# Gate and up products of two feed-forward stages as seven half-size products each, with Pool making one weight sum and the gated product

## The reference, cut to what matters

```python
h = h + mix @ w_out[l]                    # 512x1024 @ 1024x1024
hn = rms_norm_2(h, ffn_norm[l])
gu = hn @ w_gate_up[l]                    # 512x1024 @ 1024x5632
h = h + (jax.nn.silu(gu[..., :D_FF]) * gu[..., D_FF:]) @ w_down[l]
```

## Time and profile before

| | |
|---|---|
| median of 3 runs | 3445.44 us (3439.52 to 3446.58) |
| the profiled execution: its own time | 3438.87 us |
| its span, first to last instruction | 3437.1 us (1.8 us lie around it) |
| TensorE busy, DVE busy, ACT busy, Pool busy in it | 89%, 40%, 32%, 7% |
| mean granted TensorE clock | 0.958 of full |
| the two feed-forward stages | about 2240 to 2700 us and 3020 to 3437 us of the span |

### The profile page before, as it was taken

One profiled execution on the slowest core, in us unless ns is written; L12 is line 12 of the kernel. 1 busy time (PEld: TensorE's weight loads), 2 busy tenths in 40 slices (PEclk: granted clock), 3 DMA queues, 4 the chain that ended last, 5 costly groups with the idle time before them and its releaser, 6 DMA issues. The chain is left out here.

```text
span 3437.1 us, 44411 instructions
## 1 busy us (share of the span) xinstructions
PE 3069.4 (89%) x17561; PEld 2178.1 (63%) x17561; DVE 1387.9 (40%) x2258; ACT 1115.5 (32%) x1938; POOL 250.7 (7%) x278
## 2 busy tenths in 40 slices
PE   7999999999698878887887698889999998889999
PEld 5777888878533333333333485868888775778887
DVE  6872566663430000000000467553332467553332
ACT  4672666762200000000000435432222336332222
POOL 0000332210000000000000000300000000300000
PEclk9999999999899999999999799999999998999999
DMA  5322222234699999999998520023333320023332
GB/s 135 89 76 80 74 68 68 74 91 136 251 379 429 429 429 429 430 429 429 429 429 357 157 74 13 6 93 98 96 95 104 94 57 1 20 92 96 98 98 92
DMA packets 361295, 612.37 MB, mean 178 GB/s; under 512 B 73952, under 2 KB 308224, under 8 KB 336384
## 3 DMA queue, kind: packets, MB, share of 16 engines
q1 hardware_dynamic: 351152, 598.72, 47.3%
q0 software_dynamic: 9216, 8.42, 0.7%
q10 hardware_dynamic: 720, 2.36, 0.2%
HBM read 605.23 MB, written 23.07 MB: 183 GB/s over the span
## 5 line engine op out<-in xcount | busy, mean ns | idle before, releaser
L268 ACT ACTIVATE f_hi<-f_raw 128x1024 fp32r<-128x1024 f32 x148 | 156.6, 1059 | 516.2 <-PE ff_bk L328 516.0
L1888 PE MATMUL ex_up<-ex_W,ex_XT 128*64 128x512 f32 x1024 | 249.9, 644 | 76.2 <-DMA ex_W<-in_w_expert_up_dram 76.2
L1888 PE MATMUL ex_gp<-ex_W,ex_XT 128*64 128x512 f32 x1024 | 241.3, 625 | 59.2 <-DMA ex_W<-in_w_expert_gate_dram 57.8
L326 PE MATMUL ff_bk<-h_b_hi,f_hi 128*128 128x512 f32 x704 | 276.1, 392 | 2.8 <-DVE h_b_lo L3860 2.8
L327 PE MATMUL ff_bk<-h_b_lo,f_hi 128*128 128x512 f32 x704 | 275.5, 391 | 0.0
L328 PE MATMUL ff_bk<-h_b_hi,f_lo 128*128 128x512 f32 x704 | 275.3, 391 | 0.0
L277 DVE TENSOR_TENSOR f_lo<-f_raw,f_hi 128x1024 fp32r<-128x1024 f32 x148 | 180.5, 1223 | 208.4 <-ACT f_hi L268 208.0
L1917 PE MATMUL ex_yp<-ex_W,ex_hT 128*64 128x512 f32 x1024 | 228.5, 598 | 34.3 <-DMA ex_W<-in_w_expert_down_dram 21.8
L1931 DVE TENSOR_TENSOR ex_hid<-ex_sg,ex_up 128x512 f32<-128x512 f32 x32 | 22.0, 688 | 580.7 <-PE ex_up L1888 580.7
L1888 PEld LDWEIGHTS ex_up<-ex_W,ex_XT 128*64 128x64 f32 x1024 | 89.6, 147 | 235.7 <-issue 235.7
L1888 PEld LDWEIGHTS ex_gp<-ex_W,ex_XT 128*64 128x64 f32 x1024 | 88.0, 144 | 211.3 <-issue 209.5
(11 more groups left out here) (612 smaller groups left out, 6305.8 us busy)
## 6 DMA issues: line engine op xcount, KB each, us to landing
ex_W<-in_w_expert_up_dram SPq DMA_DIRECT2D x64, 2048.0 KB, 37.6
ex_W<-in_w_expert_down_dram SPq DMA_DIRECT2D x64, 2048.0 KB, 38.4
ex_W<-in_w_expert_gate_dram SPq DMA_DIRECT2D x64, 2048.0 KB, 37.6
b_raw<-in_w_in_dram SPq DMA_DIRECT2D x88, 512.0 KB, 3.8
f_raw<-in_w_gate_up_dram SPq DMA_DIRECT2D x88, 512.0 KB, 3.7
f_raw<-in_w_down_dram SPq DMA_DIRECT2D x44, 512.0 KB, 3.5
m_raw<-in_w_in_dram SPq DMA_DIRECT2D x20, 512.0 KB, 4.1
m_early<-in_w_in_dram SPq DMA_DIRECT2D x20, 512.0 KB, 4.0
```

What stands on the lines that cost most here:

```text
L268: a.activation(self.hi[n % self.SLOTS][:, to], self.raw[n % self.RAW][:, at], ACT.Copy).then_inc(self.cast, 1)
L326: pe.matmul(out, a[0], b[0], start=first, stop=False)
L1888: ins = pe.matmul(ps[part[e], :], XT[b][:, q, part[e]], row_view(slots[e], KD)[:, q, :], start=(q == 0), stop=(q == KD - 1))
```

## The change

The product of the turned tokens and the weights of one block is seen as a 2x2 by 2x2 product: tokens in halves of 256 and features of the input in halves of 512 on one side; on the other side the upper and lower half of the gate tile and of the up tile. Winograd's form of Strassen's method makes it from seven products of half size (p1 to p7) in place of eight. The product of a half is 4 rows-of-128 times `mm3`, 12 matmuls with 256 tokens moving; a block takes 7 x 12 = 84 matmuls of 256 columns.

New work for it:

- On the token side, once a stage: 14 groups of four transposes (`turn_middle(g)`) and 14 pairs `turned_hi`, `turned_lo` in place of 8, and two calls of `make_sums` (on DVE; each one subtraction over 1024 columns and two `scalar_tensor_tensor` over 512, with drains).
- On the weight side, per block u (a gate tile and an up tile): four sums of 512 columns (s3, s2, s4 on DVE, s1 on Pool), all with both inputs in SBUF, and splits of three 1024-column pairs (the gate tile, Q1, Q3) and of one 512-column tile (s2): four ACT casts and four DVE subtractions.
- After the products of block u: `keep` (ACT copies the 256 columns of p1 out of PSUM) and `join` (DVE: four additions out of PSUM, of 512, 256, 512 and 512 columns, with three drains), then `Silu` on ACT and the gated product on Pool (`gate_f`), 512 columns, both inputs in SBUF, into `raw_f`.
- The split of f (`make_f_hi`, `make_f_lo`, 22 of each) moves from the gate phase into the down phase, four of them ahead of the first down tile; the down tiles for the first column half are taken in the order `FIRST_DOWN`, and the signs of the last adds change (`ALU.subtract`).
- Gate and up tiles no longer go through `Stream` but through `GateWeights`, with four raw buffers; its loads wait for the split that frees the buffer.
- Pool's instructions wait only for their operands.

The diff, cut to its core:

```diff
+class GateWeights:
+    RAW = 4
+        order = [("p1", 0), ("p2", 0), ("p7", 0), ("p6", 0), ("p3", 0), ("p4", 0), ("p1", 1), ("p5", 0)]
+        for u in range(1, units):
+            order += [(n, u + (n == "p1")) for n in ("p7", "p6", "p3", "p2", "p1", "p4", "p5") if u + (n == "p1") < units]
+    def operand(self, n, u):
+        pair, half = {"p1": (self.g_slots[u % 2], 0), "p2": (self.g_slots[u % 2], 1), "p7": (self.q1, 0), "p3": (self.q1, 1),
+                      "p5": (self.q3, 0), "p4": (self.q3, 1), "p6": (self.s2, 0)}[n]
+    def load(self, sp, g):
...
+            sp.wait_ge((self.q1_split, self.q3_split)[g % 2], u - 1)
+    def sum_s3(self, v, u):
...
+        v.tensor_tensor(g[:, 0:T], g[:, 0:T], up[:, 0:T], ALU.add).then_inc(self.s3_ready, 1)
+    def sum_s1(self, p, u):
+        p.wait_ge(self.s3_ready, u + 1)
+        p.tensor_tensor(up[:, 0:T], up[:, 0:T], up[:, T:], ALU.add).then_inc(self.s1_ready, 1)
+    def sum_s2(self, v, u):
+        if u > 0:
+            self.wait_used(v, "p6", u - 1)
+        v.drain()
+        v.tensor_tensor(self.s2_sum(u)[:], g[:, 0:T], up[:, T:], ALU.add).then_inc(self.s2_ready, 1)
+    def sum_s4(self, v, u):
+        v.tensor_tensor(g[:, T:], g[:, T:], self.s2_sum(u)[:], ALU.add).then_inc(self.s4_ready, 1)
+    def g_hi(self, a, u):
+        self.wait_loaded(a, 2 * u)
...
+            self.wait_used(a, "p2", u - 2)
...
+    def q1_hi(self, a, u):
+        a.wait_ge(self.s4_ready, u + 1)
...
+            self.wait_used(a, "p3", u - 1)
...
+    def q3_hi(self, a, u):
+        a.wait_ge(self.s1_ready, u + 1)
...
+            self.wait_used(a, "p5", u - 1)
...
+    def s2_hi(self, a, u):
+        a.wait_ge(self.s2_ready, u + 1)
...
 def stage_ffn(...)
   TensorE
-                for m in range(BLOCKS):
-                    for j in range(2):
...
-                        for q in range(KD):
-                            ins = mm3(pe, bk[4 + 2 * j + m % 2][:], W.tile(n, q), both(h, q), q == 0, q == KD - 1)
+                def gate_product(n, u):
...
+                    for q in range(4):
+                        at_q = slice(q * P, (q + 1) * P)
+                        ins = mm3(pe, out, (hi[:, at_q], lo[:, at_q]), both(hc[n], q), q == 0, q == 3)
+                    ins.then_inc(G.used, 1)
+                for n, u in G.order:
+                    if u == 0 and n == "p7":
+                        for g in range(4, 8):
+                            turn_middle(g)
+                    elif u == 0 and n in ("p6", "p3", "p4"):
+                        for g in {"p6": (8, 9), "p3": (10, 11), "p4": (12, 13)}[n]:
+                            turn_middle(g)
...
+                    gate_product(n, u)
   ACT
+                for u in range(BLOCKS - 1):
+                    if u > 0:
+                        G.q3_hi(a, u)
+                        gate_silu(u - 1)
+                    G.s2_hi(a, u + 1)
+                    if u + 2 < BLOCKS:
+                        G.g_hi(a, u + 2)
+                    G.q1_hi(a, u + 1)
+                    keep(u + 1)
   DVE, from the last projection product on
+                add(1, 0); G.sum_s3(v, 0); scale(0); G.sum_s2(v, 0); add(1, 1); G.sum_s4(v, 0); scale(1); add(1, 2)
+                turned_lo(0, 1); add(1, 3); scale(2); turned_lo(2, 3); scale(3); make_sums(0, 1); G.q1_lo(v, 0)
+                turned_lo(4, 5); G.s2_lo(v, 0); turned_lo(6, 7, 8, 9); G.q3_lo(v, 0); turned_lo(10, 11); G.g_lo(v, 1); turned_lo(12, 13)
+                def join(u):
+                    G.wait_used(v, "p5", u)
+                    v.wait_ge(kept, u + 1)
...
+                    v.tensor_tensor(quarters[:, 0:2, :], over(first[u % 2][:]), pairs(b[1][:]), ALU.add)
+                    v.drain()
+                    v.tensor_tensor(quarters[:, 2, :], quarters[:, 1, :], b[3][:, 0:2 * P], ALU.add)
+                    v.drain()
+                    v.tensor_tensor(quarters[:, 1::2, :], quarters[:, 1:3, :], over(b[0][:, 2 * P:]), ALU.add)
+                    v.drain()
+                    v.tensor_tensor(quarters[:, 1:3, :], quarters[:, 1:3, :], pairs(b[2][:]), ALU.add).then_inc(joined, 1)
+                for u in range(BLOCKS - 1):
+                    if u > 0:
+                        join(u - 1)
+                    G.sum_s3(v, u + 1)
+                    G.sum_s2(v, u + 1)
+                    if u > 0:
+                        G.q3_lo(v, u)
+                    G.sum_s4(v, u + 1)
+                    G.s2_lo(v, u + 1)
+                    if u + 2 < BLOCKS:
+                        G.g_lo(v, u + 2)
+                    G.q1_lo(v, u + 1)
+                join(20); G.q3_lo(v, 21); make_f_lo(0 to 3); W.make_lo(v, DOWN); W.make_lo(v, DOWN + 1); make_f_lo(4, 5); join(21)
   Pool
+                def gate_f(u):
+                    p.wait_ge(sig_ready, u + 1)
+                    p.tensor_tensor(raw_f[:, u, :], z[u % 2][:, 0:T], z[u % 2][:, T:], ALU.mult).then_inc(f_ready, 1)
+                G.sum_s1(p, 0)
+                for u in range(BLOCKS - 1):
+                    G.sum_s1(p, u + 1)
+                    if u >= 1:
+                        gate_f(u - 1)
```

More of the change, by code:

```diff
@@ L3542, in stage_ffn @@
         at = k.next_left()
-        fT = k.pair(f"fT{l}", BLOCKS, ctx)
-        mixT = [x[:, 0:KD, :] for x in fT]
+        room = k.pair(f"fT{l}", BLOCKS, ctx)
+        rows_at = at + BLOCKS * T * 4
+        raw_f = k.over(f"ff{l}_raw_f", [P, BLOCKS, T], F32, at)
+        fT = (room[1], room[0])
+        mixT = [x[:, 0:KD, :] for x in room]
         xs = k.over(f"ff{l}_xs", [P, NT, D], F32, at + KD * T * 4)
+        wrow = k.over(f"ff{l}_wrow", [P, D], F32, at + 2 * KD * T * 4)
+        sums = [k.over(f"ff{l}_sums{i}", [P, 4 * T], F32, where) for i, where in enumerate((at + 2 * KD * T * 4 + 4 * D, at))]
@@ new lines, in stage_ffn @@
+        G = GateWeights(k, l, W, gates, rows_at, above, BLOCKS)
+        high = {"p1": here, "p7": here + 8192, "p2": here + 2 * 8192, "p5": above, "p6": above + 8192, "p3": above + 2 * 8192, "p4": above + 3 * 8192}
+        hc = {i: tuple(k.over(f"ff{l}_hc_{i}_{n}", [P, 4, 2 * P], F32R, x + 4096 * n) for n in range(2)) for i, x in high.items()}
+        small = here + 3 * 8192
+        first = [k.over(f"ff{l}_first{i}", [P, 2 * P], F32, small + 512 + 1024 * i) for i in range(2)]
+        tiny = lambda n, shape, x: k.over(f"ff{l}_" + n, shape, F32, x)
@@ L3665, in _ @@
+                pe.wait_ge(joined, BLOCKS - 1)
+                for i, r in enumerate(FIRST_DOWN):
+                    pe.wait_ge(f_lo, 2 * i + 2)
+                    rows(DOWN + i, 0, i, DR - 1, fT, r)
+                pe.wait_ge(joined, BLOCKS)
                 for r in range(DR - TAIL):
@@ new lines, in _, with gate_silu @@
+                turned_hi(6)
+                turned_hi(7)
+                keep(0)
+                turned_hi(8)
+                turned_hi(9)
+                G.q3_hi(a, 0)
+                turned_hi(10)
+                turned_hi(11)
+                G.g_hi(a, 1)
+                turned_hi(12)
+                turned_hi(13)
+                def gate_silu(u):
+                    a.wait_ge(joined, u + 1)
+                    a.activation(z[u % 2][:, 0:T], z[u % 2][:, 0:T], ACT.Silu).then_inc(sig_ready, 1)
@@ L3768, in last_square @@
+                last = BLOCKS - 1
+                G.q3_hi(a, last)
+                gate_silu(last - 1)
+                for i in range(4):
+                    make_f_hi(i)
+                down_hi(0)
+                down_hi(1)
+                for i in range(4, 6):
+                    make_f_hi(i)
                 def last_square(c, t):
@@ L3843, in _, with add @@
                 mix_lo_of(7)
-                def add(c, t, tile, readies):
+                def add(c, t, tile, readies, op=ALU.add):
                     if t < NT - 1:
@@ new lines, in _ @@
+                scale(0)
+                G.sum_s2(v, 0)
+                add(1, 1, last, 3)
+                G.sum_s4(v, 0)
+                scale(1)
+                add(1, 2, last, 3)
+                turned_lo(0)
+                turned_lo(1)
+                add(1, 3, last, 3)
+                scale(2)
+                turned_lo(2)
+                turned_lo(3)
+                scale(3)
+                v.drain()
+                make_sums(v, 0)
+                make_sums(v, 1)
+                G.q1_lo(v, 0)
@@ L3898, in _ @@
+                last = BLOCKS - 1
+                join(last - 1)
+                G.q3_lo(v, last)
+                for i in range(4):
+                    make_f_lo(i)
+                W.make_lo(v, DOWN)
+                W.make_lo(v, DOWN + 1)
+                make_f_lo(4)
+                make_f_lo(5)
+                join(last)
                 for n in range(2 * DR):
                     W.make_lo(v, DOWN + 2 + n)
+                    for i in range(2 * n + 6, min(2 * n + 8, BLOCKS)):
+                        make_f_lo(i)
+                    if n == DR - 1:
+                        v.wait_ge(f_ready, BLOCKS)
```

(2 more changed lines are left out.)

333 lines of the change are left out of this document (236 added, 97 removed).

## The result

The changed kernel takes 3459.8 us (median of 5 runs, 3459.6 to 3465.8), the kernel before, beside it, 3444.1 us (5 runs, 3439.5 to 3446.6): a ratio of 1.0052, interval 1.0037 to 1.0066. It is slower by 0.5%. The forecast was 3442 us, no change that shows. The time lies within the range of 3418 to 3462, by 2 us; the sign was missed.

The account below looks back on a forecast made before the run. DVE was taken to bound the changed gate phase: 41.2 us start, 19 turns of 10.54, then 9.9 and 8.5 make 259.9 us a layer against 261.5. That is 3 us less for both layers: 3442 us, range 3418 to 3462.

Parts of the forecast that it names:

- Pool, 512 columns: Gate phase: each of Pool's two products of 512 columns was to take 1.27 us, interpolated between 256 and 1024 columns.
- DVE's turn without Pool: Gate phase: DVE's work for one block's round of its loop, without delay from Pool, 8.6 us.
- the collision with s2: Gate phase: a Pool instruction beside s2, behind a drain, was to cost DVE 0.85 to 1.01 us, taken as 0.93.
- the collision with Q3's low part: Gate phase: a Pool instruction beside Q3's low part was to cost DVE 1.01 us.
- turn: Gate phase, one block's round: DVE's 8.6 plus 1.94 us for Pool, 10.54 us, above TensorE's 9.90.
- start, zero to p7 of block 1: From the first add of the second column half to block 1's p7: 41.2 us, between 38 and 43.
- blocks 20 and 21: End of the gate phase: block 20 at TensorE's 9.9 us, block 21 with six products at 8.5 us.
- balance at 10.63: Length of a block's round at which the change breaks even; each 0.1 us of it is 3.8 us of kernel.
- Rival 1: Gate phase: Pool costs DVE nothing, rounds of 9.90 us, 27.6 us less in all, 3418 us; chance 0.13.
- Rival 2: Gate phase: Pool's instructions take 1.04 us, rounds of 10.08 us, 21 us less, 3425 us; chance 0.20.
- Rival 3: Gate phase: each collision costs its whole 1.27 us, rounds of 11.14 us, 20 us more, 3465 us; chance 0.27.
- TensorE's block of 9.90: Gate phase: 84 matmuls of 256 columns at 0.1179 us take 9.90 us a block, in place of 10.88.

Follow-up runs that it names:

- hold_both: Changed kernel with both Pool instructions of a block waiting until Q1's low part is made, to run beside the join: 3403.9 us, ratio 0.9888 to the kernel before.
- hold_s1: Changed kernel with Pool's s1 waiting until Q1's low part is made, the f product free and first in Pool's queue: 3416.3 us, ratio 0.9921.
- hold_f: Changed kernel with Pool's f product waiting until Q1's low part is made, s1 left free: 3420.4 us, ratio 0.9939.
- f_twice: Changed kernel with Pool issuing each f product twice, a drain between the two: 3504.9 us, ratio 1.0175.
- s2_later: Changed kernel with s2's low part moved behind the gate tile's low part in DVE's order: 3458.8 us, ratio 1.0041.
- dve_both: Changed kernel with s1 and the f product made by DVE, Pool keeping only s1 of block 0: 3417.4 us, ratio 0.9916.
- s1_dve: Changed kernel with s1 made by DVE behind s2, Pool having only the f product, free: 3435.8 us, ratio 0.9975.
- hold_again: The same kernel as hold_both, measured once more: 3403.4 us, ratio 0.9881.

## Why the prediction missed the sign

Right were the mechanism and the order of the waits. DVE became the bound, TensorE's regular wait is before p7 and ends with the low part of Q1, Pool's two instructions meet s2 and Q3's low part, and PSUM inputs are spared (hold_both). By the steps of the sum, second layer:

| term | predicted | measured |
|---|---|---|
| Pool, 512 columns | 1.27 | 1.28 to 1.29 |
| DVE's turn without Pool | 8.6 | 8.81 |
| the collision with s2 | 0.93 | 1.14 |
| the collision with Q3's low part | 1.01 | 1.10 |
| turn | 10.54 | 11.05 |
| start, zero to p7 of block 1 | 41.2 | 39.5 |
| 19 turns | 200.3 | 209.9 |
| blocks 20 and 21 | 18.4 | 19.1 |
| a layer | 259.9 | 268.4 |

**The step that failed is the size of the collision**, "of 1.27 then 1.01" and "beside s2 (between 0.85 and 1.01, I take 0.93)": 0.30 of the 0.51 us that the turn was short. I had read 0.78 of 1.04 in the earlier trace rows and carried the difference over to 1.27. At this length the runs give Pool's 1.28 to 1.29 less 0.14 to 0.21 us (1.14 and 1.10 in the changed kernel, 1.10 in hold_s1, 1.13 in hold_f, 1.08 in f_twice). The discount for s2 "behind a drain" had no ground: where the drain holds s2 back, Pool begins 0.01 to 0.02 us ahead of it and s2 bears all. The other 0.2 us is a wait that I did not read in the code and priced at nothing, s2's low part on s4's semaphore: 0.18 us, gone in s2_later. With a balance at 10.63 and 3.8 us of kernel for each 0.1, half a microsecond was enough to turn the sign: 0.51 x 38 = 19 us, less 3 for the shorter starts.

The remainder is small. The start had fewer waits than the 3.3 us I allowed. Blocks 20 and 21 took 19.1: block 20's turn is 10.34, still DVE's and not TensorE's 9.90. In the first layer three slow turns (12.08, 11.70, 11.40) add 2.0 us. The first two are TensorE's clock. It had stood idle for 3.51 us before p7 of block 1 in both layers, but only in the first did the granted clock fall with it, to half, the 1.2 GHz level, as the windows from that p7 over one turn show (first layer, then second), and DVE's s2 had to wait for p6 of block 1:

```profile
2329.39:2341.78 12.39, 12.39 (x85) 12.39 (x86) 8.45 (x11) 4.55 (x6) 2.51 (x2) 0.76 0.30 86
...
3101.48:3112.53 11.05, 10.19 (x85) 9.79 (x85) 10.63 (x12) 5.16 (x7) 3.00 (x2) 1.00 0.33 96
```

```profile
2334.98 0.72 DVE L3635 TENSOR_TENSOR gw_s_sum<-f_raw 128x512 f32<-128x512 f32 x1 [2.42 <-PE ff_bk L329]
```

In s2_later the same befell the second layer (a turn of 12.84 us at a mean granted clock of 0.76). The prediction allowed for slow products only ahead of p7 of block 1. In the third slow turn DVE stops for 0.43 us before the last addition of a join, at 2388.1, and no wait explains it. The same stop stands before the same addition, in the first layer, in seven of the nine other runs with the changed code (all but dve_both and s1_dve), with Pool's work held or not. Its cause is open.

**The rivals.** Rival 1 (Pool costs nothing) fell here, though hold_both shows that it holds in the right place. Rival 2 fell with Pool's 1.28. Rival 3 came within 0.1 us of the turn (11.14) and 5 us of the time (3465), but not by its own working: each collision costs less than 1.27, and the missed wait made up for it. With the true 8.81 its price would have given 11.35. By the Trainium skill, "SBUF — State Buffer", section "SBUF: two separate sides", the loser is blocked for the whole instruction. That is 0.14 to 0.21 us too hard for each collision measured here; for the two of a turn it gives 2.54 against 2.24, as far above as my reading of the earlier trace rows, 1.94, was below. The same page, section "Who interferes with whom", has issue order and not the shape of the instruction decide who blocks whom; the Trainium skill agrees in this with hold_s1, where Pool, waiting since before DVE's next instruction started, had the ports first.

**A second wrong size had no effect.** TensorE's block of 9.90 is 9.52 when its step is 0.113. As DVE set the turn, it changed nothing in the changed kernel; it does in hold_both, which by my sum would have been a turn of 9.90 and gave 3404 us, 40 us less than the kernel before and 56 less than the change. It is the fastest kernel of this study: the seven products pay, and issuing Pool's work as early as its operands allow is what takes it away.

## What to carry to other kernels

An engine that shares a port with the bound one should not start as early as it can, but where the bound engine reads PSUM or waits; one wait on a semaphore was worth 56 us here, and doing the work on the bound engine itself 42. When a forecast lies within a few tenths of a microsecond of the point of balance of a loop, sum the starts of neighbours with all their waits, read the collision at both ends of its error, and give the sign no more trust than that. An order of instructions is good only for the engine that is late: the same swap helped with DVE as the bound and hurt without.

## What was not expected of the hardware

- A run of 256-column matmuls, each with its own load, steps at 0.113 or at 0.118 us at a granted clock of 1.00 (hold_again: 885 and 851 in 100 us), and may go over to the other step at a pause or at a single longer step, 0.206 us in hold_again and 0.130 to 0.136 in hold_s1. For a kernel bound by them that is up to 19 x 0.37 = 7 us a layer.
- A Pool instruction that waits for the shared ports gets in between two DVE instructions though DVE's next has started already, and that one then lasts its own time and 1.10 us more (hold_s1), where Pool's undisturbed length is 1.29.
- DVE loses 0.18 us of its overlap when an instruction waits on the semaphore of the one right ahead of it (0.78 against 0.60 between starts of 512 columns, s2_later).
- After the same idle time of 3.51 us TensorE's granted clock was half in the first layer of the changed kernel, from 2328.5 to 2335.2 us, and 1.00 in the second; the slow stretch cost two turns together 1.7 us.
